# One core, two transformer blocks with a mixture of 32 experts: ranks and gather ahead, and the first sum behind expert 28

## What is computed

```python
h = modulate(rms_norm(x, g_ffn[l]), sh_f, sc_f)
x = x + gt_f[:, None, :] * moe(h, w_router[l], b_router[l], w1[l], b1[l], w2[l], b2[l])
return rms_norm(x, g_final)

def moe(h, ...):                       # T = 256 tokens, 32 experts, D = 1024
    logits = xf @ w_router + b_router
    top_val, top_idx = lax.top_k(logits, 4)
    gates = softmax(top_val)
    # for every expert e, over the tokens that chose it:
    u = xb @ w1[e] + b1[e]             # 1024 x 2048 weights, 8 MB
    glu, lin = minimum(u[:, ::2], 7), clip(u[:, 1::2], -7, 7)
    a = glu * sigmoid(1.702 * glu) * (lin + 1)
    y += gate * (a @ w2[e] + b2[e])    # 1024 x 1024 weights, 4 MB
```

## Time and profile before

| what | us |
|---|---|
| runs, median of 3 (lowest, highest) | 1846.49 (1844.59, 1846.79) |
| profiled execution | 1849.55 |
| its span, first to last instruction | 1847.7 |
| TensorE busy | 1787.4 (97%) |
| VectorE, ScalarE busy | 815.6, 511.5 |
| moved by DMA | 568.88 MB |

### The profile page before, as it was taken

How to read it: one execution, slowest core, us unless ns; L and a number is a source line. 1 busy time by engine, 2 the same in 40 slices (tenths; PEclk the granted TensorE clock), 3 DMA queues, 4 the chain that set the end, 5 groups by cost and what they waited for, 6 DMA issues and landing times.

```text
span 1847.7 us, 27459 instructions
## 1 busy us (share of the span) xinstructions
PE 1787.4 (97%) x11187; PEld 1215.1 (66%) x11188; DVE 815.6 (44%) x1363; ACT 511.5 (28%) x845; POOL 36.6 (2%) x59
## 2 busy tenths in 40 slices
PE   6999999999998999999999999999999999999997
PEld 6988899999997899899844434434434434343342
DVE  4555668688774544547512322322322313222232
ACT  5555665444433454455300000000000000000001
POOL 2000000000000000000000000000000000000000
PEclk9999999999997999999999999999999999999999
DMA  7433447678782744449689999999999999999996
GB/s 242 130 129 115 135 139 251 206 251 273 274 297 92 239 160 154 146 142 350 256 363 426 428 429 428 429 428 429 428 429 428 429 428 429 428 429 428 429 427 263
DMA packets 148523, 568.88 MB, mean 308 GB/s; under 512 B 6048, under 2 KB 102408, under 8 KB 123104
## 3 DMA queue, kind: packets, MB, share of 16 engines
q1 hardware_dynamic: 140336, 536.60, 73.6%
q0 software_dynamic: 8112, 31.20, 4.9%
HBM read 566.71 MB, written 3.43 MB: 309 GB/s over the span
## 4 chain that ended last, share of the span: by engine, by line
PE 77%; DMA 17%; DVE 3%; ACT 2%; issue 1%; SPq 0%; DVEq 0%; ACTq 0%
PE banks L2233 18%; PE banks L1803 8%; DMA s_ring<-in_w_mlp 8%; PE banks L1805 8%; PE banks L1804 8%; PE banks L2258 8%; DMA s_W<-in_w_mlp 6%; PE banks L2270 5%; PE banks L1963 3%; PE banks L1965 3%; PE banks L1964 3%; PE banks L2217 2%; PE banks L1761 1%; PE banks L2242 1%; DMA s_ring<-in_w_ffn_up 1%
## 5 line engine op out<-in xcount | busy, mean ns | idle before, releaser
L2233 PE MATMUL banks<-s_ring,s_W 128*64 128x512 f32 x1360 | 304.9, 596 | 10.6 <-DMA s_ring<-in_w_mlp 9.7
L2233 PEld LDWEIGHTS banks<-s_ring,s_W 128*64 128x64 f32 x1360 | 93.0, 137 | 207.8 <-issue 178.2
L1100 ACT ACTIVATE s_W<-s_W 128x512 f32<-128x512 f32 x32 | 20.2, 630 | 742.1 <-DVE s_W L1668 742.1
L1657 DVE TENSOR_TENSOR s_W<-banks,s_W 128x512 f32<-128x512 f32 x32 | 22.1, 692 | 416.1 <-PE banks L2258 416.1
L2233 PE MATMUL banks<-s_W 128*64 128x512 f32 x688 | 154.3, 596 | 5.0 <-DMA s_W<-in_w_mlp 5.0
L1404 DVE TENSOR_TENSOR r_w2l<-s_ring,r_w2h 128x1024 fp32r<-128x1024 f32 x96 | 117.3, 1223 | 94.2 <-ACT r_w2h L949 94.0
L2258 PE MATMUL banks<-s_ring,s_W 128*64 128x512 f32 x704 | 155.6, 594 | 0.0
L1171 DVE TENSOR_TENSOR r_w2l<-s_ring,r_w2h 128x1024 fp32r<-128x1024 f32 x88 | 106.6, 1221 | 77.3 <-ACT r_w2h L767 65.2
L1636 DVE TENSOR_TENSOR s_W<-banks,s_W 128x512 f32<-128x512 f32 x128 | 82.1, 683 | 131.0 <-PE banks L2217 131.0
L1803 PE MATMUL banks<-r_x2h,r_w2h 128*128 128x256 f32 x448 | 130.8, 292 | 4.9 <-DVE r_x2l L1420 4.9
L2270 PEld LDWEIGHTS banks<-s_W 128*128 128x128 f32 x1024 | 116.7, 192 | 23.6 <-issue 23.6
(11 more groups left out here) (430 smaller groups left out, 3408.5 us busy)
## 6 DMA issues: line engine op xcount, KB each, us to landing
s_ring<-in_w_mlp SPq DMA_DIRECT2D x125, 2048.0 KB, 33.0
s_W<-in_w_mlp SPq DMA_DIRECT2D x62, 2048.0 KB, 32.3
s_ring<-in_w_in SPq DMA_DIRECT2D x62, 1024.0 KB, 5.2
s_ring<-in_w_ada POOLq DMA_DIRECT2D x24, 1024.0 KB, 9.4
s_ring<-in_w_ffn_gate SPq DMA_DIRECT2D x11, 1024.0 KB, 5.5
s_ring<-in_w_ffn_up SPq DMA_DIRECT2D x11, 1024.0 KB, 10.6
s_ring<-in_w_ffn_down SPq DMA_DIRECT2D x5, 2048.0 KB, 10.0
s_ring<-in_w_gate SPq DMA_DIRECT2D x8, 1024.0 KB, 5.7
```

The costliest lines, as they stand in the source:

```text
L2233: last = mm(pb[b][64 * h:64 * h + 64, :], XgT[:, 2 * c + k, :], piece(n, 2)[:, k, 1024 * h + 512 * b:1024 * h + 512 * b + 512], start=Fals ...
```

## The change

- **Ranks ahead.** The four banks of token-major copies are made in the order 0, 2, 1, 3 instead of 0, 1, 2, 3, and the rank matmuls are put ahead of the last of them.
- **Gather in halves.** The gather of expert 0 waits for the first two copies for its first four blocks, and for all four only for the others. It waits no more for `spread_kept`.
- **Gate spread, bias scaling and gates behind expert 0.** `spread` goes behind expert 0's matmuls on TensorE (banks 6 and 7), its copies behind expert 0's sigmoid on ScalarE, and `gates()` and the scaling of the b2 rows behind `shifted()` and behind expert 0 on VectorE. The scaled rows get a buffer of their own (`b2s`), and `gatT`, `gat4` move to the constants' buffer.
- **First sum behind expert 28** (`LATE = E - 3` = 29). It is no copy by ScalarE any more but two steps in the manner of a scatter: for each half of the tokens 8 identity matmuls and 2 matmuls with b2 into banks 6 and 7, then `add_up` on VectorE. The first values of `acc` now come from expert 0: its two `add_up` copy instead of adding.
- The loops on VectorE and ScalarE end at expert 28 and not 30. From there on the counts on `sc_mm` and `acc_done` are two higher (`sums`).

The diff, cut to its core:

```diff
+LATE = E - 3
@@ ScalarE
-        for b in range(4):
-            act.wait_ge(S["ht_mm"], b + 1)
+        for n, b in enumerate((0, 2, 1, 3)):
+            act.wait_ge(S["ht_mm"], n + 1)
...
-        for b in range(2):
-            act.wait_ge(S["spread"], b + 1)
-            v = slice(64 * b, 64 * b + 64)
-            act.activation(gty[v, :], pb[2 - b][v, :], ACT.Copy).then_inc(S["spread_kept"], 1)
         act.wait_ge(S["route"], 4)
         act.activation(gts, gts, ACT.Exp).then_inc(S["log_exp"], 1)
...
         expert(0, True, False)
-        first_sum()
+        for b in range(2):
+            act.wait_ge(S["spread"], b + 1)
+            v = slice(64 * b, 64 * b + 64)
+            act.activation(gty[v, :], pb[6 + b][v, :], ACT.Copy).then_inc(S["spread_kept"], 1)
+        act.wait_ge(S["b2_scaled"], 1)
         expert(1, True, True)
-        with act.Fori(2, E - 1) as e:
+        with act.Fori(2, LATE) as e:
+            expert(e, True, True)
+        act.wait_ge(S["gt_mm"], 1)
+        act.activation(gatT, pb[5][:, 0:T], ACT.Copy).then_inc(S["gt_kept"], 1)
+        for e in range(LATE, E - 1):
             expert(e, True, True)
@@ VectorE
                 shifted().then_inc(S["xg"], 1)
                 choose_u(e + 1)
+                if isinstance(e, int) and e == 0:
+                    gates()
...
-        gates()
+        expert(0, True, False)
         nc.vector.memset(taken, 0.0).then_inc(S["round"], 1)
...
-        tt(b2q, b2q, gty, ALU.mult).then_inc(S["b2_scaled"], 1)
-        expert(0, True, False)
-
-        dve.wait_ge(S["acc_init"], 4)
+        tt(b2s, b2q, gty, ALU.mult).then_inc(S["b2_scaled"], 1)
         expert(1, True, True)
-        with dve.Fori(2, E - 1) as e:
+        with dve.Fori(2, LATE) as e:
+            expert(e, True, True)
+        for r in range(2):
+            dve.wait_ge(S["acc_done"], 2 * LATE - 2 + r)
+            add_up(r, 2 * LATE - 1 + r)
+        for e in range(LATE, E - 1):
             expert(e, True, True)
@@ TensorE
+            pe.wait_ge(S["selt"], LATE - 1)
             for t in range(2):
-                last = nc.tensor.transpose(pb[2][:, P * t:P * t + P], gat4[:, t, :], ident)
+                last = nc.tensor.transpose(pb[5][:, P * t:P * t + P], gat4[:, t, :], ident)
             last.then_inc(S["gt_mm"], 1)
...
+            for r in range(2):
+                pe.wait_ge(S["acc_done"], 2 * LATE - 2 + r)
+                for h in range(2):
+                    for j in range(4):
+                        mm(pb[6 + h][:, P * j:P * j + P], hx[:, 4 * h + j, P * r:P * r + P], ident, start=j == 0, stop=False, skip_group_check=True)
+                pe.wait_ge(S["gt_kept"], 1)
+                pe.wait_ge(S["b2_scaled"], 1)
+                for h in range(2):
+                    v = slice(E * (2 * h + r), E * (2 * h + r) + E)
+                    last = mm(pb[6 + h], gatT[v, P * r:P * r + P], b2s[v, :], start=False, stop=True, skip_group_check=True)
+                last.then_inc(S["sc_mm"], 1)
...
                 for k in range(KT):
+                    if isinstance(e, int) and e == 0:
+                        pe.wait_ge(S["ht_kept"], 2 if k < 4 else 4)
...
+        expert(0, True, False)
+        for b in range(2):
+            spread(6 + b, modT[:, 40:48], b)
         pe.wait_ge(S["spread_kept"], 2)
-        expert(0, True, False)
-        first_sum()
         expert(1, True, True)
         with pe.Fori(0, 9) as i:
             for j in range(3):
                 expert(i * 3 + (2 + j), True, True, (i, 2 + j))
-        for e in (E - 3, E - 2):
+        first_sum()
+        for e in range(LATE, E - 1):
             expert(e, True, True)
```

More of the change, by code:

```diff
@@ L404, in program @@
     yv, aT, li, sg = W[:, 0:512], area(W, 512, 4, P), W[:, 1024:1536], W[:, 1536:2048]
-    gatT, gat4, diag = W[:, 0:T], area(W, 768, 2, P), area(W, 1024, KT, P)
+    gatT, gat4, diag = cst[:, C_NEGM:C_NEGM + T], area(cst, C_NTRI, 2, P), area(W, 1024, KT, P)
+    b2s = W[:, 6144:6656]
     shift = vx[:, 48:56]
@@ L429, in program @@
         "act_step", "dve_step", "ht_mm", "ht_kept", "route_mm", "log_exp", "route", "rank_done",
-        "gt_mm", "gt_kept", "spread", "spread_kept", "b2_scaled", "h_mm", "acc_init",
+        "gt_mm", "gt_kept", "spread", "spread_kept", "b2_scaled",
         "selu", "selg", "selt_mm", "selt", "gath", "xg", "used", "u_read", "u_sig", "a_mid", "a_done", "at_mm", "at", "yv_done",
@@ L543, in since, with sums @@
             eng.wait_ge(S[name], n)
+    def sums(e):
+        return e * 2 + (2 if isinstance(e, int) and e >= LATE else 0)
     def further(eng, each, begin=None):
@@ L1094, in expert @@
                 act.wait_ge(S["selt_mm"], e)
-                since(act, "sc_mm", e * 2 - 2)
+                since(act, "sc_mm", sums(e) - 2)
                 act.activation(selT, pb[5][:, 0:T], ACT.Copy).then_inc(S["selt"], 1)
@@ L1635, in add_up @@
                 v = acc[:, r, 512 * h:512 * h + 512]
-                last = tt(v, pb[bank + h], v, ALU.add)
+                if n <= 2 and isinstance(n, int):
+                    last = nc.vector.tensor_copy(v, pb[bank + h])
+                else:
+                    last = tt(v, pb[bank + h], v, ALU.add)
             last.then_inc(S["acc_done"], 1)
@@ L1655, in weighed @@
                 dve.wait_ge(S["used"], 6 * E if final else e * 6 + (4 if late else 2))
-                since(dve, "sc_mm", e * 2 - 2)
+                since(dve, "sc_mm", sums(e) - 2)
                 tt(yv, pb[2], gty, ALU.mult).then_inc(S["yv_done"], 1)
-                since(dve, "acc_done", e * 2 - 2)
-                add_up(0, e * 2 - 1)
+                since(dve, "acc_done", sums(e) - 2)
+                add_up(0, sums(e) - 1)
             if prev and not late:
@@ L1681, in expert @@
                 weighed()
-                add_up(1, e * 2)
+                add_up(1, sums(e))
         choose_u(0)
@@ L1705, in _ @@
         expert(E, False, True)
[L1706 removed]
+        dve.wait_ge(S["acc_done"], sums(E))
         def next_round(r):
@@ L2171, in _ @@
         last.then_inc(S["route_mm"], 1)
-        for b in range(4):
+        for n, b in enumerate((0, 2, 1, 3)):
+            if n == 3:
+                pe.wait_ge(S["route"], 5)
+                mm(pb[0][:, 0:E], tri, msk[:, 0, :], start=True, stop=True)
+                mm(pb[0][:, E:2 * E], ones[:, :], msk[:, 0, :], start=True, stop=False)
+                mm(pb[0][:, E:2 * E], tri, msk[:, 1, :], start=False, stop=True)
+                mm(pb[0][0:1, 2 * E:3 * E], ones[:, 0:1], msk[:, 0, :], start=True, stop=False)
+                mm(pb[0][0:1, 2 * E:3 * E], ones[:, 0:1], msk[:, 1, :], start=False, stop=True).then_inc(S["route_mm"], 1)
             for j in range(4):
@@ L2189, in spread @@
             last.then_inc(S["spread"], 1)
-        for b in range(2):
-            spread(2 - b, modT[:, 40:48], b)
-        pe.wait_ge(S["ht_kept"], 4)
         def first_sum():
             pe.wait_ge(S["route"], 6)
+            pe.wait_ge(S["selt"], LATE - 1)
             for t in range(2):
-                last = nc.tensor.transpose(pb[2][:, P * t:P * t + P], gat4[:, t, :], ident)
+                last = nc.tensor.transpose(pb[5][:, P * t:P * t + P], gat4[:, t, :], ident)
             last.then_inc(S["gt_mm"], 1)
[L2201 to L2210, removed]
+            for r in range(2):
[9 more added lines that the diff above has]
+                last.then_inc(S["sc_mm"], 1)
         def scatter(r, n, bank=6):
@@ L2296, in expert @@
                 since(pe, "selt", e)
-                scatter(0, e * 2 - 2)
+                scatter(0, sums(e) - 2)
             if cur and not late:
@@ L2303, in expert @@
                 else:
-                    scatter(1, e * 2 - 1)
+                    scatter(1, sums(e) - 1)
+        expert(0, True, False)
+        for b in range(2):
+            spread(6 + b, modT[:, 40:48], b)
         pe.wait_ge(S["spread_kept"], 2)
-        expert(0, True, False)
-        first_sum()
         expert(1, True, True)
```

12 lines of the change are left out of this document (2 added, 10 removed).

## The result

The changed kernel takes 1849.35 us (median of 20 runs, 1844.34 to 1858.89), the kernel before 1846.13 (20 runs beside them, 1841.16 to 1849.99). The ratio of the times is 1.0026, 95% interval 1.0016 to 1.0037: slower by 0.26%, some 3 to 5 us. The forecast was no change.

A forecast was written before the change was run, and what follows sets the result against it. The prediction took the weight stream to bound the experts, set by the first two up products, and TensorE the end behind 1790. It summed -4.5 (2.8 + 1.76) and +4.6 (7.6 - 2.98) to +0.1: 1846.6 us, range 1842.6 to 1850.0.

The forecast's parts named there:

- The head, -2.8: Start up to expert 0's product: earlier ranks and gather, gates beside the product; up product at about 918.6, 2.8 us earlier.
- Between expert 0 and 1, -1.76: TensorE from expert 0 to expert 1: 5.01 us of work becomes 3.25, including 1.25 idle for ScalarE; 1.76 us less.
- such a fall in the first sum alone: Rival: TensorE's clock falls in the two waits of the sum at expert 29, adding 1.5 us, 1848.1; chance 0.18.
- The first sum, +7.6: Ahead of expert 29: two steps and two waits for VectorE take TensorE 7.6 us, bounds 5.0 to 9.1.
- wait for VectorE: Behind iteration 28's second scatter: TensorE goes on 1.53 us later, with two transposes (0.37) inside.
- a step: Each half at expert 29: 8 residual and 2 bias matmuls, half of 3.57 plus half of 1.07, 2.32 us.
- the exchange between the steps: At expert 29, between the two halves: VectorE must add the first, 0.1 + 1.28 + 0.05 = 1.43 us.
- What hides it, -2.98: From expert 29 to 1790: two iterations each wait 1.49 us for the stream, hiding 2.98 and leaving 4.6.
- the case that the end hangs on the last transfer: Rival: last down product waits for the last bytes, so the late sum hides and 4.5 stays; 1842.0, chance 0.15.
- Loops that end earlier: VectorE and ScalarE leaving loops at expert 28 cost nothing; rival of a code fetch stall, 1848.2, chance 0.04.
- The sum: Whole kernel: -4.5 at the start and +4.6 at the end give +0.1 us, they cancel at 1846.6; chance 0.50.

## Why the prediction was wrong

**The head, -2.8.** Right. Ranks 0.65 earlier, gather bound by `selU` and not by the halves of `htok`, gates beside the product. The up product of expert 0 moved by 2.65.

**Between expert 0 and 1, -1.76.** Right in size: 5.01 became 3.17 when the clock held (27.01 - 9.90 behind the copies, less the product's 13.94). The first up product of expert 1 came 4.45 us earlier (31.85 against 36.30), and the stream 4.55 earlier (817.91 against 822.46), one for one, as forecast. What the step missed is what an idle gap of 1.2 us can do to the granted clock. It was written down as idle time only; in three of five executions the clock was at 0.50 for some 6 us behind it, and 3.2 of the 4.5 us were gone. The rivals looked for such a fall in the first sum alone, at 1.5 us with a chance of 0.18; there it came in the other two executions, at 1.6.

**The first sum, +7.6.** This is the step that failed. It measured 9.27. Term by term, forecast and chain: wait for VectorE 1.53 and 1.59; a step 2.32 and 3.13, then 3.11; the exchange between the steps 1.43 and 1.44. The two steps carry all of the 1.6 that were missing. They were taken as half of the earlier trace rows, 3.57 / 2 + 1.07 / 2. But the four bias matmuls of the kernel before took 1.07 together, and two of them take 1.06. At the residual's rate (16 matmuls of 128 columns in 3.57, 0.22 each) one of 512 columns would take about 0.9 us, an estimate, and four in a row 3.6. So the four ran beside each other, and so did the two; they are 32 rows deep and lie on different rows of the array. The two of a scatter, 64 rows deep, take as long (1.06 in the earlier trace rows). Taking two away from such a group saved nothing. The eight residual matmuls take 2.05 behind a wait and 1.98 without one, not 1.79. A group of instructions was divided by its count where it had a length of its own.

**What hides it, -2.98.** Right. From 9.27 it leaves 6.3; the end moved from 115.0 (the execution of the kernel before without a fall there) to 121.6, which is 6.6. That nothing behind iteration 30 hides more was right too: the case that the end hangs on the last transfer is excluded by the run with the sum at 23, which is 6.6 faster, and by the chain of the changed kernel, in which no transfer stands behind 1726. Loops that end earlier cost nothing in this place, since both waits for VectorE have the length forecast, within 0.1. The rule on taken branches (the Trainium skill, Runtime: NRT & Kernel Launch, Instruction fetch mechanics) had nothing to act on here, and the trace agrees with it so far.

**The sum.** -4.55 + 6.6 is +2.1 instead of +0.1, and that is about what the two kernels differ by at equal clock (some 2 us in the one group of runs, 1.9 to 3.9 in all). Part of the rest of the measured 3 to 5 goes with the clock: of five executions of the changed kernel every one had a fall in the changed stretches, 3.2 or 1.6 us each. In two of the kernel before there was one at the gather of expert 0 (2.3) and one at the last scatters (1.4), so the net share of the clock is some 0.7 us in these seven. Up to 1 or 2 us of the ratio, and the rare executions above 1855, are left unexplained.

**Still open.** Why the stream loses 1.3 to 1.9 us between experts 23 and 28 when the first sum stands at 23. With the changed head it reaches iteration 28 at 819.8, 818.6 and 819.0 in the three kernels, where the same heads with the sum at 29 have 817.9 to 818.3 and 817.3. Their instruction queue moved 1.05 MB instead of 0.93, which at 428 GB/s is 0.3 us. It moved the additional part in that very stretch, behind the end of the loops: from 1555 to 1725 the run with the sum at 23 has

```profile
q8 instruction: 7, 0.11, 0.3%
```

and the changed kernel has no such packet there. A piece has landed only when all of its packets have, so a few packets ahead of some of them could cost more than their share of the bytes; that is a conjecture, and no run tells it from others.

## What to carry to other kernels

Work that is moved to where an engine waits for a stream is hidden by the waits that still lie behind it, not by those in front. Here it is 1.49 us an iteration, so a sum of 9.3 us wants seven iterations behind it, and had two. When part of a group of matmuls is priced, ask what its length comes from: the small ones here, on different rows of the array, ran together, and half of them took as long as all. And a new wait of TensorE on another engine, of 1.2 us here, is to be priced with the chance that the clock falls behind it, and against the gaps that are there already: what it costs is the difference between a fall here and a fall there.

## What the runs showed of the hardware

An idle gap of 1.17 us ahead of a gather was followed by half clock in three of five executions of one program. In the changed kernel's rows the clock fell at 934, 2.2 us after TensorE had gone on (931.74), and stayed at 0.50 beyond 940, although TensorE was busy all that time. In the two gaps of 1.16 and 1.46 us of the first sum it fell in the other two executions: in one of them it is at 0.50 from 1737 into 1740, and the second step takes longer (3.02 and 1.77 instead of 2.05 and 1.13):

```profile
1736.11 3.02 PE L2211 MATMUL banks<-s_cst,s_hT 128*128 128x128 f32 x16 [1.46 <-DVE s_W L1640]
1739.05 1.77 PE L2216 MATMUL banks<-s_W,s_cst 32*128 32x512 f32 x4
```

No execution had both, and each had one. Gaps of the same length (1.16 and 1.46) stood in the first sum at expert 23, and there the clock stayed at 1.00 in all three executions that have them. So one program pays 1.6 us in one execution and 3.2 in another with nothing changed in its order, and single executions of it are compared only stretch by stretch, at equal clock.
